# A two-block model on one core: stage ends by token tiles, and the first up chunk of both blocks in two passes

## The reference

```python
h = rms_norm(x, norm1_g); proj = h @ w_in
y_rnn = (rg_lru(causal_dwconv(rx, ...), ...) * gelu(rgate)) @ w_rnn_out
y_attn = nsa(q, kc, vc, ks, vs, kw, vw, ...) @ w_attn_out
x = x + (sigmoid(mg_rnn) * y_rnn + sigmoid(mg_attn) * y_attn) @ w_out
up = causal_dwconv(rms_norm(x, norm2_g) @ w_up, ffn_conv_w, ffn_conv_b)
gate, val = split(up, 2); x = x + (gelu(gate) * val) @ w_down
# second block
mix = hybrid_mixer(x, w_in_2, ...)        # attention over 8 heads, and a gated unit
x = layer_norm(ALPHA * x + mix, ln1_g, ln1_b)
x = layer_norm(ALPHA * x + (silu(x @ w_gate) * (x @ w_up_2)) @ w_down_2, ln2_g, ln2_b)
```

## Time and profile before

| what | value |
| --- | --- |
| median of 3 runs | 867.5 us (864.85 to 868.99) |
| the profiled execution, its own time | 861.49 us |
| its span, first to last instruction | 859.8 us |
| PE busy | 839.4 us |
| DVE busy | 577.7 us |
| ACT busy | 490.8 us |
| mean granted clock | 0.994 |

### The profile page before, as it was taken

One profiled execution on the slowest core, in us unless ns is written; L12 is line 12 of the kernel. 1 busy time (PEld: TensorE's weight loads), 2 busy tenths in 40 slices (PEclk: granted clock), 3 DMA queues, 4 the chain that ended last, 5 costly groups with the idle time before them and its releaser, 6 DMA issues.

```text
span 859.8 us, 12671 instructions
## 1 busy us (share of the span) xinstructions
PE 839.4 (98%) x5224; PEld 736.4 (86%) x5224; DVE 577.7 (67%) x739; ACT 490.8 (57%) x718; POOL 37.7 (4%) x44
## 2 busy tenths in 40 slices
PE   9999999999999999999999999999999999999995
PEld 8999979798898998788888888878787888888884
DVE  4672578696865766588877886766666664564555
ACT  5563468777856544466656665536653554554542
POOL 0100200000000000100000000022121000000001
PEclk9999999999999999999999999999999999999998
DMA  7636424142334667245565556475345455556441
GB/s 270 203 121 233 157 97 167 50 146 97 119 118 148 235 208 268 98 157 192 191 199 193 196 184 207 147 269 196 98 150 194 148 197 194 176 180 232 151 144 49
DMA packets 22217, 145.68 MB, mean 169 GB/s; under 512 B 2576, under 2 KB 3088, under 8 KB 7696
## 3 DMA queue, kind: packets, MB, share of 16 engines
q1 hardware_dynamic: 20736, 139.56, 46.7%
q10 hardware_dynamic: 1424, 5.31, 1.7%
HBM read 143.82 MB, written 1.05 MB: 168 GB/s over the span
## 4 chain that ended last, share of the span: by engine, by line
PE 85%; DVE 7%; ACT 4%; issue 2%; DMA 1%; POOL 1%; SPq 0%; DVEq 0%; POOLq 0%; ACTq 0%
PE PS L1512 18%; PE PS L1515 9%; PE PS L1524 8%; PE PS L1525 8%; PE PS L1526 8%; PE PS L1500 8%; PE PS L1501 8%; PE PS L1502 8%; DVE WL L934 2%; PE PS L1606 1%; PE PS L1550 1%; PE PS L1583 1%; DVE CG L1335 1%; ACT WH L566 1%; PE PS L1745 1%
## 5 line engine op out<-in xcount | busy, mean ns | idle before, releaser
L934 DVE TENSOR_TENSOR WL<-RAW,WH 128x2048 fp32r<-128x2048 f32 (+2 forms) x129 | 288.6, 2238 | 81.4 <-ACT WH L566 81.3
L566 ACT ACTIVATE WH<-RAW 128x2048 fp32r<-128x2048 f32 (+2 forms) x129 | 241.5, 1874 | 82.6 <-PE PS L1526 31.4
L1500 PE MATMUL PS<-BHL,WH 128*128 128x256 f32 (+2 forms) x424 | 120.6, 284 | 1.0 <-ACT TI L719 1.0
L1502 PE MATMUL PS<-BHL,WL 128*128 128x256 f32 (+2 forms) x424 | 119.5, 282 | 0.0
L1501 PE MATMUL PS<-BHL,WH 128*128 128x256 f32 (+2 forms) x424 | 119.5, 282 | 0.0
L1324 DVE TENSOR_TENSOR HLS<-PS,HLS 128x512 f32<-128x512 f32 x46 | 31.8, 692 | 102.5 <-ACT HLS L841 101.6
L1512 PE MATMUL PS<-CHL,WH 128*128 128x512 f32 x384 | 96.5, 393 | 0.4 <-DVE WL L934 0.3
L1512 PE MATMUL PS<-BHL,WH 128*128 128x512 f32 x352 | 88.5, 394 | 0.0
L1500 PEld LDWEIGHTS PS<-BHL,WH 128*128 128x128 f32 (+2 forms) x424 | 79.6, 188 | 2.9 <-issue 2.6
L1512 PEld LDWEIGHTS PS<-CHL,WH 128*128 128x128 f32 x384 | 69.3, 189 | 14.6 <-DVE CHL L941 0.8
L1501 PEld LDWEIGHTS PS<-BHL,WH 128*128 128x128 f32 (+2 forms) x424 | 79.6, 188 | 0.0
(11 more groups left out here) (277 smaller groups left out, 1393.5 us busy)
## 6 DMA issues: line engine op xcount, KB each, us to landing
RAW<-in_w_stream SPq DMA_DIRECT2D x109, 1024.0 KB, 4.9
RAW<-in_w_stream SPq DMA_DIRECT2D x12, 1008.0 KB, 4.8
RAW<-in_w_stream SPq DMA_DIRECT2D x8, 768.0 KB, 4.3
WF<-in_w_stream SPq DMA_DIRECT2D x2, 1024.0 KB, 5.4
LN<-in_ln ACTq DMA_DIRECT2D x2, 1024.0 KB, 6.0
WF<-in_w_stream SPq DMA_DIRECT2D x4, 420.0 KB, 3.2
X<-in_x SPq DMA_DIRECT2D x2, 512.0 KB, 4.1
X<-in_x ACTq DMA_DIRECT2D x1, 1024.0 KB, 4.9
```

Of the source, the lines that this page charges most:

```text
L566: eng.activation(WH[:, c % NSLOT, 0:CHUNKS[c][2]], raw(c), ACT.Copy).then_inc(w_hi, 1)
L934: eng.tensor_tensor(WL[:, c % NSLOT, 0:CHUNKS[c][2]], raw(c), f32(WH[:, c % NSLOT, 0:CHUNKS[c][2]]), ALU.subtract).then_inc(w_lo, 1)
L1500: eng.matmul(out, wh, H[0:parts, k, :], start=(k == 0), stop=False)
L1502: last = eng.matmul(out, wl, H[0:parts, k, :], start=False, stop=(k == nk - 1))
```

## The change

The diff's core follows; left out are the helpers that only carry it (`tile_transposes`, `tile_hi` and `tile_lo` transpose and split one token tile, in four half-size pieces per engine; `wo_part`, `wo2_part` and `down_half` are calls of `t_part`).

1. **Start.** The first chunk is fetched by two transfers of half a chunk, and ACT waits for each half by itself. The kv chunks have one more place to arrive (`RAW3`).
2. **Order on DVE.** After a ri chunk the subtraction for a later chunk comes behind the next unit's maximum. In in2 chunk 7 the maximum of unit 2 comes ahead of the work on ZT, and in chunk 9 ACT copies V2's first tile ahead of the squares. PE takes unit 2 before unit 1 there. The last mg chunk uses bank 2 and waits for the last exponential, not for the gates' bank.
3. **Stage ends by tiles.** In the last two chunks of wo, dn, wo2 and dn2 PE works token tile 0 of both chunks before tile 1 of the second. The transposes of tile 0 stand among the last matmuls of tile 1. in2's first two chunks are worked as (tile 0, first half), the transposes of tile 1, (0, second), (1, first), (1, second). The clock-keeping matmuls of 12 and 2, 5, and 8 and 2 at the three seams become 2, 0 and 2.
4. **First up chunk by tiles.** Chunk 0 of up and up2 is worked by `hl_pass`: all matmuls over tile 0, then the transposes of tile 1, then all matmuls over tile 1. A high matmul moves 2 x 128 columns and a low one 128.
5. **Power.** The root of wo's norm takes one POOL instruction and not two.

```diff
         slots = list(range(NRAW)) + [NRAW] * (kind in ("up", "dn")) + [NRAW + 1] * (kind in ("up2", "dn2"))
+        slots += [NRAW + 2] * (kind == "kv")
         slot = min(slots, key=lambda n: -1 if last[n] is None else last[n])
...
-SUMS_FIRST = (("wo", 3), ("dn", N_UP // 2 - 1), ("wo2", 2))
+SUMS_FIRST = (("wo", 3), ("dn", N_UP // 2 - 1), ("in2", 9), ("wo2", 2))
...
-                    eng.dma_start(raw(c), source).then_inc(raw_in[slot], 16)
+                    if c == 0:
+                        first, second = slice(0, CHUNK // 2), slice(CHUNK // 2, CHUNK)
+                        eng.dma_start(raw(c)[:, first], source[:, first]).then_inc(w0_in, 16)
+                        eng.dma_start(raw(c)[:, second], source[:, second]).then_inc(raw_in[slot], 16)
+                    else:
+                        eng.dma_start(raw(c), source).then_inc(raw_in[slot], 16)
                 else:
...
-                power(rs1[:, t:t + 1], ss1s[:, t:t + 1], 1, DM, EPS, x1_rstd)
+                eng.tensor_tensor(rs1[:, t:t + 1], ss1s[:, t:t + 1], half[:, 0:1], ALU.pow).then_inc(x1_rstd, 1)
...
-                    if i == 3:
-                        evict_hi(CH, XT_BANKS[2], xt2_done, xt2_hi)
+                        if i == 3:
+                            if t == 1:
+                                split(c + 2)
+                            tile_hi(CH, (XT_BANKS, XT1_BANKS)[t][2], xt2_done, xt2_hi, t)
...
+                    tile_hi(BH, XT_BANKS[3], xt3_done, xt3_hi, 0)
+                    split(c + 2)
...
-                    norm_squares(0)
+                    norm_squares(0, 0)
                     eng.wait_ge(mr_ready, 4)
                     eng.dma_start(LN2[:, :, :].rearrange("p a n -> p (a n)"), A_ln2.partition_broadcast(P))\
-                       .then_inc(ln2_in, 16)
-                    evict_hi(BH, XT_BANKS[4], xt4_done, xt4_hi)
+                       .then_inc(rows_in, 16)
+                    tile_hi(BH, XT_BANKS[4], xt4_done, xt4_hi, 0)
+                    norm_squares(0, 1)
+                    split(c + 2)
+                    tile_hi(BH, XT1_BANKS[4], xt4_done, xt4_hi, 1)
...
+                    x1_sum(0)
                     if i == 3:
...
+                        x1_squares(0)
+                        x1_normed(0)
+                        tile_lo(CH, CL, XT_BANKS[2], xt2_hi, xt2_lo, 0, kps=(0, 1))
...
+                    x1_sum(1)
+                    if i == 3:
+                        tile_lo(CH, CL, XT_BANKS[2], xt2_hi, xt2_lo, 0, kps=(2, 3))
+                        x1_squares(1)
+                        x1_normed(1)
+                        tile_lo(CH, CL, XT1_BANKS[2], xt2_hi, xt2_lo, 1)
...
+                        if t == 1:
+                            split(c + 2)
+                        tile_lo(BH, BL, XT_BANKS[3], xt3_hi, xt3_lo, t)
...
+                if n == 0:
+                    residual_sum(0, 0, 1)
+                    mean(0)
+                    eng.wait_ge(gains_in, landed)
+                    gain(0)
+                    residual_sum(0, 1, 0)
+                    finish(0)
+                    tile_lo(BH, BL, XT_BANKS[4], xt4_hi, xt4_lo, 0, kps=(0, 1))
+                    residual_sum(0, 1, 1)
+                    mean(1)
+                    gain(1)
+                    tile_lo(BH, BL, XT_BANKS[4], xt4_hi, xt4_lo, 0, kps=(2, 3))
+                    finish(1)
+                    tile_lo(BH, BL, XT1_BANKS[4], xt4_hi, xt4_lo, 1)
+                else:
+                    residual_sum(1, 0, 0)
+                    residual_sum(1, 0, 1)
+                    mean(0)
+                    eng.wait_ge(gains_in, landed)
+                    gain(0)
+                    residual_sum(1, 1, 0)
+                    finish(0, (0,))
+                    residual_sum(1, 1, 1)
+                    mean(1)
+                    gain(1)
+                    finish(0, (1,))
+                    finish(1)
...
                     unit_max(u)
+                if c and CHUNKS[c - 1][0] == "ri":
+                    split(c + 1)
...
+            def hl_pass(bank, c, col0, HL, t, lo_ready=None):
+
+                s = c % NSLOT
+                tile = slice(P * t, P * t + P)
+                both = PS[:, bank, :].rearrange("p (a t) -> p a t", a=2)[:, :, tile]
+                for k in range(KD):
+                    if lo_ready is not None and k % 2 == 0:
+                        eng.wait_ge(lo_ready, 4 * t + k // 2 + 1)
+                    wh = WH[:, s, col0 + P * k:col0 + P * k + P]
+                    eng.matmul(both, wh, HL[:, k, :, tile], start=(k == 0), stop=False)
+                for k in range(KD):
+                    wl = WL[:, s, col0 + P * k:col0 + P * k + P]
+                    last = eng.matmul(PS[:, bank, tile], wl, HL[:, k, 0, tile], start=False, stop=(k == KD - 1))
                 return last
 
...
+                if m == MB_NO[AT["mg", 2 * NG - 1]]:
+                    eng.wait_ge(exp_done, NU)
...
+                    if i < 2:
+                        last = t_half(c, (b, b + 1), i, BH, BL)
+                    elif i == 2:
+                        wo_part(c, 0, 0)
+                        eng.wait_ge(w_lo, SPLIT_NO[c + 1] + 1)
+                        eng.wait_ge(m_lo, 8)
+                        wo_part(c + 1, 1, 0).then_inc(tile0_done, 1)
+                        last = wo_part(c, 0, 1)
+                    else:
+                        wo_part(c, 1, 1, (0, 1, 2))
+                        tile_transposes(XN2, XT_BANKS[2], xn2_ready, 0, 2, xt2_done, 0)
+                        last = wo_part(c, 1, 1, (3,))
                 if kind == "up":
...
+                        if i == 0:
+                            last = hl_pass(UP_BANKS[0] + v, c, 1024 * v, CHL, 1, lo_ready=(xt2_lo, None)[v])
+                        else:
+                            last = hl_tile(UP_BANKS[i % 2] + v, c, 1024 * v, CHL)
...
+                        for t in range(NT):
+                            for n in range(2):
+                                last = down_half(c, i, t, n)
+                    elif i == n_all - 2:
+
                         for n in range(2):
-                            last = t_part(PS[:, first_bank + 2 * t + n, :], c, 512,
-                                          [((2 * i + k) % NR, 1024 * k + 512 * n) for k in range(2)], AH, AL, t,
-                                          i == 0, i == n_all - 1)
-                        if i == n_all - 1 and t == 0:
-                            last.then_inc(tile0_done, 1)
+                            down_half(c, i, 0, n)
+                        if kind == "dn":
+                            down_half(c, i, 1, 0)
+                        eng.wait_ge(w_lo, SPLIT_NO[c + 1] + 1)
+                        eng.wait_ge(lo_s, 2 * i + 4)
+                        for n in range(2):
+                            last = down_half(c + 1, i + 1, 0, n)
+                        last.then_inc(tile0_done, 1)
+                        for n in range(kind == "dn", 2):
+                            last = down_half(c, i, 1, n)
+                    else:
+                        ins = down_half(c, i, 1, 0)
+                        if kind == "dn":
+                            tile_transposes(X1, XT_BANKS[3], x2_ready, 0, 1, xt3_done, 0)
+                        if kind == "dn2":
+                            ins.then_inc(tile0_done, 1)
...
+                    if i < 2:
+
+                        for t, j in (((0, 0), (0, 1), (1, 0)), ((1, 1),))[i]:
+                            eng.wait_ge(w_lo, SPLIT_NO[c - i + j] + 1)
+                            eng.wait_ge(xt3_lo, 4 * t + 2 * j + 2)
+                            last = t_part(PS[:, IN2_BANKS[0] + t, :], c - i + j, 512, [(4 * j + kk, 512 * kk) for kk in range(4)],
+                                          BH, BL, t, j == 0, j == 1)
+                            if t == 0 and j == 0:
+                                tile_transposes(X1, XT_BANKS[3], x2_ready, 0, 1, xt3_done, 1)
+                            elif t == 0:
+                                last.then_inc(tile0_done, 1)
+                    else:
+                        last = t_half(c, (IN2_BANKS[b], IN2_BANKS[b] + 1), i, BH, BL)
                 if kind == "wo2":
...
                 if kind == "wo" and i == 3:
-                    keep_clock(12, 6, BH)
-                    transposes(XN2, XT_BANKS[2], xn2_ready, xt2_done, halves=True)
-                    keep_clock(2, 2, BH)
-                if kind == "dn" and i == N_UP // 2 - 1:
-                    transposes(X1, XT_BANKS[3], x2_ready, xt3_done)
-                    keep_clock(5, 2, CH)
+                    eng.wait_ge(w_lo, SPLIT_NO[c + 1] + 1)
+                    for v in range(2):
+                        hl_pass(UP_BANKS[0] + v, c + 1, 1024 * v, CHL, 0, lo_ready=(xt2_lo, None)[v])
+                    tile_transposes(XN2, XT1_BANKS[2], xn2_ready, 0, 2, xt2_done, 1)
+                    keep_clock(2, 0, BH)
...
                 if kind == "wo2" and i == 2:
```

(27 more changed lines are left out.)

178 lines of the change are left out of this document (102 added, 76 removed).

## The result

The changed kernel took 856.77 us in the median of four runs (853.51 to 859.36), the kernel before 866.17 us in four runs beside it (863.8 to 868.99): ratio 0.9888, interval [0.9841, 0.9936], faster by 1.1%. The forecast was 857.9. Its profiled execution took 856.93 us with a span of 855.1 us, so profile against profile (859.8 us before) only 4.6 us are won, where the terms promised 9.6.

A forecast was written before the change was run, and what follows sets the result against it. PE, busy 839.4 of 859.8 us, was taken as the bound. Savings 0.9 + 3.9 + 0.9 + 2.2 + 0.9 + 0.8 = 9.6 us off the 867.5 median gave 857.9; 8-in-10 range 855 to 865.5.

The forecast's parts named there:

- Price of the narrow matmul: First up and up2 chunks: a 128-column matmul taken at 0.115 us, bounds 0.112 and 0.22; not in the trace.
- (a): Rival, chance 0.22: the 64 narrow matmuls cost 0.22 us each, 6.8 us more; 864.7 us, no change.
- (c): Rival, chance 0.08: PSUM runs of 128 columns slow every matmul of the token-tile passes; 3.6 us slower, 871.1.
- Start, 0.9: First chunk in two halves: first product at 10.8 to 10.9 instead of 11.81; 0.9 us saved, bounds 0.3 and 1.0.
- Softmax waits, 2.3 ahead of the first seam: PE waits removed: 1.3 us by DVE's maximum before its subtraction, 1.0 by the last mg chunk not awaiting the gates' bank.
- Softmax waits, 1.6 in in2: In in2: earlier maximum 0.6 us, V2's copy ahead of the squares 1.2, 0.2 given back to the later cast.
- wo to up, 0.9: Seam into the first feed-forward block: work by token tiles, first pass stalls about 0.9 us; second up chunk 0.9 earlier.
- dn to in2, 2.2: Seam out of the first feed-forward block: first two in2 chunks end at 570.9 instead of 573.0; 2.2 us saved.
- wo2 to up2, 0.9: Seam into the second block: first pass stalls about 2.3 us behind DVE, second up2 chunk at 672.4; 0.9 us saved.
- rival (b): Chance 0.11: the clock falls in a remaining stall, 1.7 us for each of one or two seams; 859.6 to 861.3.
- End, 0.8: Kernel end: last norm starts at 855.1 instead of 855.92; 0.8 us saved, bounds 0 and 1.4.

The follow-up runs named there:

- the order undone: The changed kernel with in2's softmax maximum, V2 copy, transposed weights' copy and last products in the order of before, stage 9's cast left as changed: 854.36 us, ratio 0.9897.

## Why the prediction was right, and where it was not

The time came out 1.1 us from the forecast, and "faster" was right. The sum behind it was only partly so.

- **Price of the narrow matmul**, the term in doubt: right. 0.1125 us at 128 columns, against bounds of 0.112 and 0.22; rivals (a) and (c) are out. The Trainium skill, "TensorE: Matmul & The Clock Gate", section "Back-to-back issue gap", gives about 81 ns at 128 columns. The trace disagrees: 112.5 ns. The Trainium skill, "PSUM — Partial Sum Buffer", section "Specifications (TRN2)", says that a non-contiguous access slows matmuls significantly. The trace shows nearly nothing of it for two runs of 128 columns: eight such matmuls follow each other in 1.00 us from 353.95 on, 0.125 each, against 0.12 for 256 columns without a gap.
- **Start, 0.9**: wrong, 0.0 to 0.3. Two steps failed. Half the bytes hardly land sooner, which my lower bound of 0.3 had named. And I let the first product follow PE's last transposition at once, at 10.8 to 10.9; 0.59 us lie between them even with early weights, so about 11.5 was the earliest.
- **Softmax waits, 2.3 ahead of the first seam**: mis-sized, 1.55 (317.00 to 315.45, in two profiles with no fall there), of which the ri order is 0.96 and the rest, by subtraction, the bank of the last mg chunk. All waits went; why they brought less than their length is open.
- **Softmax waits, 1.6 in in2**: 2.3. For V2 I had put the gain on the copy's place and given back 0.2 for the later cast; the later cast alone is enough for it.
- **wo to up, 0.9**: 1.5, of which the passes are 0.5. The stall was 0.3 shorter than forecast, and the second pass with what stands ahead of it 0.3 shorter too. The second up chunk started 1.8 us earlier than before, not 4.1, for the two terms ahead of it.
- **dn to in2, 2.2**: right where the race is won, 233.73 to 231.5 to 232.0 in four profiles; the changed kernel's own profile gave all of it back at the rope adds. I had not asked what an earlier cast on ACT would set free on DVE, and what that would meet, nor when in2's weights arrive: PE came to in2 5.1 us sooner and they 1.4.
- **wo2 to up2, 0.9**: the stall of 2.2 us was foreseen, and rival (b) as well: a fall behind it cost 1.6 us, for which I had put 1.7. Without a fall on either side the seam goes from 35.95 us (the kernel before, profiled again) to 35.23, 0.7 won. By my steps the second up2 chunk should have started 8.8 us earlier; it was 3.9.
- **End, 0.8**: right, 186.39 to 185.62; the last norm started at 851.28 instead of 855.92, 4.6 us earlier and not 9 to 10, for what was lost ahead of it.

So the profiles differ by 4.6 us and not by 9.6: 1.2 lost to the fall at 107 (318.20 with and 317.00 without it in the kernel before), 1.6 to that at the second seam, some 2.2 to the race, 0.9 at the start, 0.8 in the first softmax waits; and 1.7 more than forecast gained at the two seams and in in2. That the medians differ by 9.4 all the same has reasons that the forecast did not give. The times of the kernel before follow its mean clock: 860.8 to 862.3 us at 0.998, 868.9 to 869.4 at 0.984 to 0.987. A straight line through the 94 runs of all versions, one slope and a level for each, gives 1.36 us for each 0.002 of mean clock, about what one stretch of 3.41 us at 1.2 GHz is; it leaves 1.1 us of scatter. At 0.998 it puts the kernel before at 860.5 and the changed one at 853.7, 6.8 us apart, and the mean clock rose from 0.992 to 0.994, another 1.2. The stretches without their falls add up to the same, 1.55 + 1.5 + 2.3 + 0.7 + 0.8, with nothing from dn to in2, where the first profile of before won the race and that of the changed kernel lost it. In two of three profiles the kernel before lost 1.4 to 3.0 us behind its wait for V2; in ten profiles of versions without that wait this stretch took 37.77 to 37.79 us, and 38.59 with the order undone, with no fall. Subtracting from the median a sum made against one profiled execution assumed that its excess over the profile would stay; part of it, by those two profiles, was falls behind a wait that the change removed, and this made up for terms that failed. The three-run median that it started from, 867.5, was high as well: 35 later runs of the kernel before had medians of 863.3, 863.6 and 865.2. The forecast was right by luck in good part: a start that was too high and a sum that was too large.

Open: why 10 of 11 profiles of the changed versions have the fall near 107 and the kernel before one in three; the count is too small to say that the change brings it. The share of the mg bank was not tried by itself, nor were the stage ends by tiles at dn, dn2 and the two seams: their gain is read from the lengths of the stretches, and no run undoes them.

## What to carry to other kernels

When work is cut in two so that its first half can fill a wait, put what that half needs ahead of everything for the second half on the engine that serves both: here the place of two small subtractions decided whether the cut was worth nothing or 1.4 us. Ask of every wait removed which engine now starts earlier, what it will run beside, and whether the weights that it wants next arrive earlier too; and read several profiles of a kernel whose runs spread, since what one profile shows as won or lost (a fall of the clock, a race between two engines) may be the draw.

## What the hardware showed that I had not expected

- The granted clock fell for 3.41 us or twice that, 6.83, and the same stall of 2.2 us brought a fall in some executions and none in others. Matmuls of 64 columns suffer too: 32 of them took 5.59 us instead of 3.76.
- DVE's 2.29 us subtraction and GpSimd's add of 1.27 (half of the pair's 2.55) did not share time in these profiles: whichever came second was longer by most of what was left of the other, GpSimd's pair 4.63 for 2.55, DVE's 3.38 or 3.16 for 2.29.
- Half a chunk beside its other half and the next chunk landed after 6.3 to 6.8 us, and after 5.4 without them.
